# One bias matmul for gate and up, and the down bias added once through the routing weights

## The reference, cut to what matters

```
comb = sum over the chosen k of wts[t, k] * onehot(idx[t, k])        # (tokens, 32)
for e in range(32):
    gu = t @ w_gate_up[e] + b_gate_up[e]                             # 2048 columns
    gate = min(gu[:, :1024], 7);  up = clip(gu[:, 1024:], -7, 7)
    h = (up + 1) * gate * sigmoid(1.702 * gate)
    out += comb[:, e] * (h @ w_down[e] + b_down[e])
```

## Time and profile before

| what | value |
|---|---|
| median of 3 runs | 1248.34 us (1242.94 to 1248.47) |
| profiled execution, its own time | 1245.98 us |
| its span | 1243.9 us |
| mean granted TensorE clock | 0.994 |
| TensorE busy | 1195.3 us (96%) |
| DVE busy | 334.0 us (27%) |
| ScalarE busy | 214.9 us (17%) |
| DMA moved | 447.11 MB, mean 359 GB/s |

### The profile page before, as it was taken

How to read it: one execution, slowest core, us unless ns; L and a number is a source line. 1 busy time by engine, 2 the same in 40 slices (tenths; PEclk the granted TensorE clock), 3 DMA queues, 4 the chain that set the end, 5 groups by cost and what they waited for, 6 DMA issues and landing times.

```text
span 1243.9 us, 14181 instructions
## 1 busy us (share of the span) xinstructions
PE 1195.3 (96%) x5663; PEld 573.3 (46%) x5663; DVE 334.0 (27%) x797; ACT 214.9 (17%) x417; POOL 24.8 (2%) x56
## 2 busy tenths in 40 slices
PE   7999999999999999999999999999999999999897
PEld 5777777452443434343443433443434343434242
DVE  4444214151223132222222121232122222222223
ACT  2555502120101010000010011210100000001024
POOL 1000100000000000000000011000000000000000
PEclk9999999998999999999999999999999999999999
DMA  9834673469899999999999999999999999999931
GB/s 303 286 135 143 187 299 135 169 248 393 349 429 428 428 428 426 429 429 428 428 427 429 429 426 427 426 428 428 426 429 427 428 428 428 426 428 427 426 144 38
DMA packets 51281, 447.11 MB, mean 359 GB/s; under 512 B 7903, under 2 KB 9023, under 8 KB 26425
## 3 DMA queue, kind: packets, MB, share of 16 engines
q1 hardware_dynamic: 48752, 440.30, 85.6%
q0 software_dynamic: 2368, 6.10, 1.6%
q10 hardware_dynamic: 112, 0.03, 0.0%
HBM read 444.90 MB, written 1.88 MB: 359 GB/s over the span
## 4 chain that ended last, share of the span: by engine, by line
PE 78%; DMA 18%; DVE 1%; ACT 1%; POOL 1%; issue 1%; SPq 0%; DVEq 0%; ACTq 0%
PE ps L1056 26%; DMA ring<-in_w_gate_up 16%; PE ps L744 16%; PE ps L1074 14%; PE ps L934 7%; PE ps L1088 4%; PE ps L892 2%; PE ps L1169 2%; DMA out<-work 2%; PE ps L1014 1%; PE ps L1004 1%; PE ps L738 1%; POOL out L713 1%; PE ps L780 1%; PE ps L1176 1%
## 5 line engine op out<-in xcount | busy, mean ns | idle before, releaser
L1056 PE MATMUL ps<-ring,work 128*64 128x512 f32 x2016 | 441.9, 593 | 12.8 <-DMA ring<-in_w_gate_up 12.4
L1056 PEld LDWEIGHTS ps<-ring,work 128*64 128x64 f32 x2016 | 144.1, 137 | 291.4 <-issue 257.7
L1074 PE MATMUL ps<-ring,work 128*64 128x512 f32 x1024 | 229.1, 600 | 5.9 <-ACT work L1371 5.1
L744 PE MATMUL ps<-work,ring 128*128 128x288 f32 x752 | 186.2, 410 | 0.0
L744 PEld LDWEIGHTS ps<-work,ring 128*128 128x128 f32 x752 | 143.8, 192 | 41.0 <-issue 1.7
L1074 PEld LDWEIGHTS ps<-ring,work 128*64 128x64 f32 x1024 | 71.7, 138 | 144.8 <-issue 131.6
L1869 DVE TENSOR_SCALAR work<-ps 128x512 f32<-128x512 f32 x32 | 22.1, 692 | 382.1 <-PE ps L1056 382.1
L934 PEld LDWEIGHTS ps<-work,x_tok 128*128 128x128 f32 x768 | 91.9, 197 | 15.3 <-issue 14.4
L934 PE MATMUL ps<-work,x_tok 128*128 128x128 f32 x768 | 95.4, 284 | 1.7 <-ACT work L1365 1.3
L1421 ACT ACTIVATE work<-work 128x512 f32<-128x512 f32 x32 | 20.2, 630 | 428.0 <-DVE work L1869 428.0
L1722 DVE TENSOR_SCALAR work<-iota_slot,slot,stat 128x64 f32<-128x64 f32 x96 | 24.4, 310 | 217.3 <-PE ps L1074 217.0
(11 more groups left out here) (230 smaller groups left out, 590.7 us busy)
## 6 DMA issues: line engine op xcount, KB each, us to landing
ring<-in_w_gate_up SPq DMA_DIRECT2D x126, 2048.0 KB, 26.9
ring<-in_w_down SPq DMA_DIRECT2D x64, 2048.0 KB, 30.7
ring<-in_w_in SPq DMA_DIRECT2D x7, 2048.0 KB, 14.2
ring<-in_w_proj_b SPq DMA_DIRECT2D x2, 2048.0 KB, 7.9
ring<-in_w_proj_a SPq DMA_DIRECT2D x2, 2048.0 KB, 9.1
ring<-in_w_out SPq DMA_DIRECT2D x2, 2048.0 KB, 12.1
ring<-in_w_ple_gate SPq DMA_DIRECT2D x4, 1024.0 KB, 29.6
ring<-in_w_in SPq DMA_DIRECT2D x2, 1024.0 KB, 9.1
```

The source lines that it names most:

```text
L744: mm = pe.matmul(out(b), lhs, rhs, start=(k == 0), stop=(k == len(pairs) - 1))
L1056: mm = pe.matmul(ps[half(g), b, :], xg[:, k, i % 2, :], block(k % 2, at + 512 * g), start=False, stop=(k == KC - 1))
L1074: mm = pe.matmul(ps[half(g), b, :], hT[:, 4 * j + k, :], whole_piece(s)[:, at + 512 * g:at + 512 * g + 512], start=False, stop=(4 * j + k ...
```

## The change

The gate and up biases are laid out anew. `pick_gu` gets 128 columns, 64 for the first half of the output and 64 for the second, and the 96 bias rows are split by half: of each part's 32 rows the first 16 belong to columns 0 to 511 and the other 16 to columns 512 to 1023. A row holds two experts (e and e + 16, by `share`). One matmul with 128 columns then writes both halves. The loads of the biases go from 6 to 12 smaller ones, the three parts are 2048 and not 3072 wide, and `expert_col` is built with 18 copies and not 6.

The down bias leaves the experts. Its rows go as float32 to 32 partitions of the `yb` buffer (`down_bias`), loaded on POOL's queue once the channel block b is through. TensorE turns the routing weights `comb` (`turn_weights`, after expert 0's gate and up products), ScalarE copies them (`keep_weights`), TensorE multiplies them with `down_bias` after expert 1's gate and up products and ahead of the gather (`weigh_down_bias`), and DVE adds the result to `x_tok` and writes `x2` (`add_down_bias`), after expert 1's `pick_expert` and ahead of `gathered`. `copy_residual`, `x1_copied`, `pick_d` and its semaphore go. The down product's first matmul now starts the bank itself.

```diff
 # plan_psum
+    take("combT", B_S)
+    for i, bank in enumerate(B_Y):
+        take(("shift", i // 2, i % 2), bank)
 # buffers
-        bias_parts = flat_w[:, W + 3 * D:W + 3 * D + 3 * D // 2].bitcast(BF16)
+        bias_parts = flat_w[:, W + 3 * D:W + 4 * D].bitcast(BF16)
+        down_bias = flat_w[BIAS_ROWS:P, W + 3 * D:W + 4 * D]
+        combT = sel_wT[BIAS_ROWS:P, :, :]
 # POOL's queue
             for i in range(BIAS_PARTS):
-                pool.dma_start(bias[NE * i:NE * i + NE, 0:2 * D], b_gate_up[0]).then_inc(bias_landed, 16)
-                pool.dma_start(bias[NE * i:NE * i + NE, 2 * D:3 * D], b_down[0]).then_inc(bias_landed, 16)
+                for g in range(2):
+                    at = NE * i + HALF_E * g
+                    for s in range(2):
+                        pool.dma_start(bias[at:at + HALF_E, D * s:D * s + D].rearrange("e (k c) -> e k c", k=2),
+                                       b_gate_up[0, HALF_E * s:HALF_E * s + HALF_E, :]
+                                       .rearrange("e (k h c) -> e k h c", k=2, h=2)[:, :, g, :]).then_inc(bias_landed, 16)
+            wait_filled(pool, ("b", KC - 1))
+            pool.dma_start(down_bias, b_down[0]).then_inc(down_bias_landed, 16)
 # TensorE, begin_sums
-                for g in range(2):
-                    pe.matmul(ps[half(g), b, :], pick[0:BIAS_ROWS, :],
-                              bias_parts[0:BIAS_ROWS, at + 512 * g:at + 512 * g + 512],
-                              start=True, stop=False)
+                pe.matmul(ps[:, b, :], pick_gu[0:BIAS_ROWS, :],
+                          bias_parts[0:BIAS_ROWS, D * share + at:D * share + at + 512], start=True, stop=False)
+            def turn_weights():
+                pe.wait_ge(comb_ready, 1)
+                b = begin("combT")
+                for t in range(TT):
+                    mm = pe.matmul(ps[BIAS_ROWS:P, b, t * P:t * P + P], comb[:, t, :], ident[:], start=True, stop=True)
+                mm.then_inc(filled[b], 1)
+            def weigh_down_bias():
+                pe.wait_ge(down_bias_landed, 16)
+                wait_read(pe, "combT")
+                for t in range(TT):
+                    for h in range(2):
+                        b = begin(("shift", t, h)) if t < TT - 1 or h == 0 else b
+                        mm = pe.matmul(ps[column_half(("y", t, h)), b, :], combT[:, t, 0:ROWS[t]],
+                                       down_bias[:, 512 * h:512 * h + 512], start=True, stop=True)
+                        if t < TT - 1 or h == 1:
+                            mm.then_inc(filled[b], 1)
 # TensorE, quad, after weigh_gate_up and add_pair, ahead of gather
+                    if isinstance(n, int) and n == 0:
+                        turn_weights()
+                    if isinstance(n, int) and n == 1:
+                        weigh_down_bias()
...
-                    pe.wait_ge(pick_d_ready, n + 1)
-                    begin_sums("out", n, pick_d[:], 2 * D)
+                    begin_chunk(pe, "out", n)
 # ScalarE, ahead of keep_hidden(0)
+            def keep_weights():
+                b = wait_filled(act, "combT")
+                nc.scalar.copy(combT.rearrange("p t s -> p (t s)"), ps[BIAS_ROWS:P, b, 0:TT * P]).then_inc(emptied[b], 1)
 # ScalarE, after keep_hidden(1)
-                    if begins and i == 1:
-                        copy_residual()
 # DVE
+            def add_down_bias():
+                for t in range(TT):
+                    for h in range(2):
+                        b = wait_filled(dve, ("shift", t, h if t < TT - 1 else 0))
+                        own = slice(512 * h, 512 * h + 512)
+                        ins = V.tensor_tensor(x2[0:ROWS[t], t, own], x_tok[0:ROWS[t], t, own],
+                                              ps[column_half(("y", t, h)), b, :], ALU.add)
+                        if t < TT - 1 or h == 1:
+                            ins.then_inc(emptied[b], 1)
-                    pick_expert(pick_d[:], e, scaled=ends and i >= 2).then_inc(pick_d_ready, 1)
...
+                    if isinstance(n, int) and n == 1:
+                        add_down_bias()
```

More of the change, by code:

```diff
@@ L93 @@
 BIAS_ROWS = BIAS_PARTS * NE
+HALF_E = NE // 2
 V_GMIX, V_CW, V_CB, V_BRA, V_BRX, V_LAM, V_PS, V_GMOE, V_GPLE = 0, 8, 40, 48, 56, 64, 72, 80, 88
@@ L240, in hybrid_layer @@
         lam = carve(12 * KC).rearrange("p (i c) -> p i c", i=12)
-        expert_col = sb("expert_col", [P, NE + 1], BF16)
+        expert_col = sb("expert_col", [P, 2, NE + 1], BF16)
         hist = carve(KC * HIST).rearrange("p (c w) -> p c w", c=KC)
@@ L262, in hybrid_layer @@
         comb = sb("comb", [P, TT, NE])
-        pick_d = sb("pick_d", [P, CAP], BF16)
-        pick_gu = sb("pick_gu", [P, CAP], BF16)
+        pick_gu = sb("pick_gu", [P, 2 * CAP], BF16)
         slot = sb("slot", [P, TT, NCH + 4])
@@ L281, in hybrid_layer @@
         flat_w = work[:].rearrange("p a b -> p (a b)")
-        bias = flat_u[:, 0:3 * D]
+        bias = flat_u[:, 0:2 * D]
         pT = tails[:].rearrange("p i c t -> p (i c t)")[:, 0:2 * NTOK].rearrange("p (k t) -> p k t", k=2)
@@ L357, in hybrid_layer @@
         pick_gu_ready = sem("pick_gu_ready")
-        pick_d_ready = sem("pick_d_ready")
+        down_bias_landed = sem("down_bias_landed")
         sig_ready = sem("sig_ready")
@@ L370, in hybrid_layer @@
         x_cleared = sem("x_cleared")
-        x1_copied = sem("x1_copied")
         sel_w_ready = sem("sel_w_ready")
@@ L726, in _ @@
             pool.wait_ge(p_landed, 16 * 4)
+            pool.wait_ge(down_bias_landed, 16)
         @block.tensor
@@ L1008, in _, with begin_sums @@
             h_blocks = [h_fours[:, k, :] for k in range(4)]
-            def begin_sums(kind, n, pick, at):
+            def begin_sums(kind, n, share, at):
                 b = begin_chunk(pe, kind, n)
-                for g in range(2):
-                    pe.matmul(ps[half(g), b, :], pick[0:BIAS_ROWS, :],
-                              bias_parts[0:BIAS_ROWS, at + 512 * g:at + 512 * g + 512],
-                              start=True, stop=False)
+                pe.matmul(ps[:, b, :], pick_gu[0:BIAS_ROWS, :],
+                          bias_parts[0:BIAS_ROWS, D * share + at:D * share + at + 512], start=True, stop=False)
             def gather_last_tile(c0):
@@ L1075, in weigh_down @@
                                            whole_piece(s)[:, at + 512 * g:at + 512 * g + 512],
-                                           start=False, stop=(4 * j + k == KC - 1))
+                                           start=(j == 0 and k == 0), stop=(4 * j + k == KC - 1))
                     if j == 0:
@@ L1091, in add_pair, with quad @@
                             mm.then_inc(filled[bank], 1)
-            def quad(Q, late, embeds=False, last=False):
+            def turn_weights():
[14 more added lines that the diff above has]
+                            mm.then_inc(filled[b], 1)
+            def quad(Q, share, late, embeds=False, last=False):
                 for i in range(4):
@@ L1097, in quad @@
                     pe.wait_ge(pick_gu_ready, n + 1)
-                    begin_sums("gate", n, pick_gu, 0)
-                    begin_sums("up", n, pick_gu, D)
+                    begin_sums("gate", n, share, 0)
+                    begin_sums("up", n, share, 512)
                     if isinstance(n, int) and n == 0:
@@ L1127, in _ @@
             pe.wait_ge(bias_cast, BIAS_PARTS)
-            quad(0, False)
+            quad(0, 0, False)
             pe.wait_ge(passes_ready, 1)
@@ L1131, in _ @@
             with pe.Fori(1, LATE_QUAD) as Q:
-                quad(Q, False)
-            quad(LATE_QUAD, False, embeds=True)
+                quad(Q, 0, False)
+            quad(LATE_QUAD, 1, False, embeds=True)
             with pe.Fori(LATE_QUAD + 1, QUADS - 1) as Q:
-                quad(Q, True)
+                quad(Q, 1, True)
             with pe.If(more > 0):
                 with pe.Fori(0, more) as c:
-                    with pe.Fori(0, QUADS) as q4:
-                        quad(c * QUADS + q4 + (QUADS - 1), True)
-            quad(more * QUADS + (QUADS - 1), True, last=True)
+                    for share in range(2):
+                        with pe.Fori(QUADS // 2 * share, QUADS // 2 * (share + 1)) as q4:
+                            quad(c * QUADS + q4 + (QUADS - 1), share, True)
+            quad(more * QUADS + (QUADS - 1), 1, True, last=True)
             add_pair(more * PAIRS + PAIRS, True, final=True)
@@ L1302, in _ @@
                 z_gate(c)
-            act.wait_ge(bias_landed, 16 * 2 * BIAS_PARTS)
+            act.wait_ge(bias_landed, 16 * 4 * BIAS_PARTS)
             wait_filled(act, ("b", KC - 1))
@@ L1425, in quad @@
                         keep_embedding()
+                    if begins and i == 0:
+                        keep_weights()
                     keep_hidden(n)
-                    if begins and i == 1:
-                        copy_residual()
                     if i % 2 == 1:
@@ L1521, in _ @@
```

(19 more changed lines are left out.)

## The result

| | before | after |
|---|---|---|
| median of 12 runs each | 1244.86 us (1242.94 to 1248.47) | 1251.03 us (1249.72 to 1252.38) |
| profiled execution, its span | 1245.98, 1243.9 | 1249.99, 1248.3 |
| mean granted clock | 0.994 | 0.990 |

The ratio is 1.0046, with a 95% interval of 1.0035 to 1.0057: 5.7 us (4.4 to 7.1) slower, just under the 0.5% that was set as the bound for no change. With more runs the median before is 3.5 us lower than the three runs had it.

What follows compares the result with a forecast made beforehand. The weight stream was taken to bound the experts, paced by expert 1's down product. All terms were 0 except +4.8 us there: 1245.98 + 4.8 = 1250.8, said as 1251, range 1245.5 to 1256.5.

Steps and rivals of the forecast that it cites:

- The bound: End of the first half of expert 1's down product paces everything behind it; every microsecond there moves the end one for one.
- Rival C: Weight stream at 320 to 324: it makes the 4.8 us up, so the change costs nothing; 1246.0 us, chance 0.07.
- rival D: TensorE bounds the experts, so dropping the pairs is a real gain: 13 us at most, less 4.8; 1238, chance 0.02.
- TensorE's wait for hT: Experts 0 and 1: down product needs ScalarE's hT copy anyway, so dropping the bias pair gains 0 to 0.1 us.
- The term of 4.8: Expert 1: shift matmuls and DVE adds start the gather at 317.05 in place of 312.23, +4.8 us (bounds 2.9 to 9.4).
- The two limits: Expert 1's gather: TensorE free of shift matmuls at 316.9, bank 6 free of DVE's third add at 317.0; the later decides.
- with DVE as releaser: Sign of being right: expert 1's gather starts about 4.8 us later after its gate/up block, released by DVE.
- the likeliest case: Granted clock as before, with the fall at expert 0: +4.8 us, 1251 us, chance 0.42.
- A: Expert 0: clock stays at 1.00 because the gap is shorter, -2.8 us; +2.0 in all, 1248.0 or 1250.3; chance 0.33.
- B: Expert 1: clock falls at 32-row shift matmuls and a short bank 6 stop, about 3.1 us; +7.9 in all, chance 0.13.
- Gate and up biases: Every expert: one full-width matmul costs the same as two side-by-side halves; gain 0, bounds 0.43 us either way.
- The stream never runs dry again: Behind expert 1's down product: ring places come free every 3.5 us against 4.9 us to move a piece.

Runs made afterwards that it cites:

- late1: Kernel after, with the down-bias matmuls moved to pair 1's sums (expert 2), over 128 rows, 96 of them zero: 1246.50 us, 1.0006 of the kernel before.
- late_sum: The first experiment: kernel after, with the 32-row down-bias matmuls moved to expert 2 as second terms of pair 1's sums; 1249.43 us, 1.0042 of before.
- twice: Kernel after, with each of the six 32-row shift matmuls at expert 1 made twice: 1261.24 us, 1.0136 of the kernel before.
- late8: Kernel after, with the down-bias matmuls moved to pair 8's sums (expert 16), over 128 rows, 96 of them zero: 1243.97 us, 0.9993 of before.
- no_down_bias: Kernel after without any down bias or turn_weights, residual copies of the kernel before restored: 1243.77 us, 0.9996 of the kernel before.
- full_rows: Kernel after, with the six shift matmuls at expert 1 over 128 rows, 96 of them zero, in place of 32: 1248.70 us, 1.0031 of before.
- turn_only: Kernel after without the down bias, residual copies restored, but turn_weights and its copy kept with result unused: 1243.90 us, 0.9992 of before.
- before_again: The kernel before, unchanged, executed once more for its profile: 1244.02 us.
- merge_only: Kernel before with only the full-width gate and up bias matmul; down bias still a pair in each expert: 1244.93 us, 1.0005 of before.

## Why the prediction was right, and where it wasn't

**The total.** 1251.0 was forecast and 1251.03 measured; the agreement to a hundredth is luck. From the median of before as it now stands, the forecast's +4.8 would be 1249.7; the ratio says +5.7.

**The bound: right.** The end moves with the moment at which expert 1's down product frees its ring place. The part of the span behind it is 920.9 us before and 921.9 after. Less what the last expert loses to the clock, it is 920.5 to 921.1 us in eleven of the fourteen profiles, while the issue itself lies anywhere from 318.8 to 326.4. The three others are late1 (924.1) and late_sum (926.8), which ran the stream dry again, and twice (922.6), with its stop at expert 28. Rival C falls, since the added work costs 4.8 where it stood; rival D falls, since no version without the pairs is faster and 4.6 us of added work at expert 16 cost nothing (late8). no_down_bias says less than it was made for: its pairs had lain in TensorE's wait for hT, as the prediction itself had read at experts 0 and 1.

**The term of 4.8: right, and shown by itself.** full_rows minus turn_only is 4.8. The two limits, 316.9 for the matmuls and 317.0 for the third add, lay as close as the 0.13 us stop in full_rows says. In the kernel after the matmuls alone decide, since the clock makes them later, so the sign "with DVE as releaser" came only in full_rows.

**The clock: the likeliest case was wrong in both directions.** The forecast had it as before. Instead A and B both came, each near its own price (2.8 and 3.1): -2.6 at expert 0, and at expert 1 +0.9 in the shift matmuls and +2.15 in the gather. Together with the 4.6 of six matmuls at the full clock and the 0.25 of the bias matmuls that is 5.3. It lies near the forecast by chance, because the two falls nearly cancel. B came without the stop that it named as a condition: the fall began within the shift matmuls, with TensorE busy. B was given 0.13 because no busy stretch of ordinary matmuls was seen to fall, and none of them worked on 32 rows; the stretch at 27.20 did fall, but was put down to the transposes ahead of it. That reading is weaker than it looked: all fourteen profiles have those 17 transposes, near 23 us, and the clock fell behind them in six. So what keeps it up there is open too.

**turn_weights at expert 0.** Ten profiles have it there, and in nine the clock stayed up; the tenth, late_sum, had 9.51 us. Of the four without it (before, before_again, no_down_bias, merge_only) all fell. So A is right in the traces. The median doesn't show it: the same ten have the fall at the last expert in nine, at 0.7 to 1.7 us, and the four have it in none. In their two profiles that cancels: 1.7 us lost at expert 0 in no_down_bias, and 1.7 at the last expert in turn_only. What ties the two places together stays open.

**Gate and up biases: taken at 0, they cost 0.25 an expert.** The pair of halves does run side by side, as read. But the full-width form takes 0.11 more in its own matmuls and 0.15 in the block behind; the 0.25 of expert 1 reached the end. It shortens the stream's margin too, from 1.7 to 1.4 us an expert, averaged over experts 2 and 3.

**Behind the stream: a claim that was too wide.** "The stream never runs dry again" is true of both kernels, but its margin with the change is 1.7 us at the whole of expert 2 and not the 1.4 us a piece that the text compares. The forecast did not hang on it; my first experiment did, and missed by 6 us.

## What to carry to other kernels

A busy share of 96% didn't say what bounds this kernel. Find the last moment at which the weight stream is dry: here work ahead of it cost its full length, and work behind it what exceeded the margin gained since. Count that margin as stream time less TensorE time per round, and move one-time work at least so far back. Before counting a matmul as saved, look whether it stood in a wait. For a small contraction, try filling the unused rows with zeros and look at the granted clock; here that gave back 2.3 us.

## What the runs showed of the hardware that I had not expected

- Two kernels have matmuls over 32 rows in a row, and both lost the clock in them. TensorE was busy without a break and the granted clock fell from 1.00 to 0.50 (1.2 GHz) some 3.5 us into them, for about 7 us in the kernel after and 14 in twice. With the same columns over 128 rows (full_rows), and with 32 and 128 rows in turn (late_sum), it stayed at 1.00.
- Alternating matmuls of 128 and 32 rows took 1.05 us each for 0.86 (late_sum, the first eight).
- One bf16 matmul of 128 columns in place of two side by side of 64, for gate and for up, made matmuls and block together 0.25 us longer at the same clock (merge_only: 0.54 + 13.88 for 0.43 + 13.73).
- The length of an idle time did not decide whether the clock fell behind it. At expert 0 it fell in four profiles of four after 2.73 us and in one of ten after 1.96; at the last expert the idle was 2.8 us in all fourteen, and it fell in nine; ahead of expert 28's bias matmuls TensorE stood still for 1.9 to 2.5 us in all fourteen, and the clock fell in five, and in twice behind its further stop of 4.09.
